# Summing 27 conditioning chunks on VectorE inside the 512-token feed-forwards of a two-block transformer kernel

## What is computed

```python
mod_x = (jax.nn.silu(c) @ w_ada[l] + b_ada[l]).reshape(bn, 1, N_MOD, d)
mod_c = (jax.nn.silu(c_ctx) @ w_ada[l] + b_ada[l]).reshape(1, 1, N_MOD, d)
h_x = _half_ffn(h_x, norm_g[l, 0], mod_x[:, :, 0], mod_x[:, :, 1], mod_x[:, :, 2], ffn1_up[l], ffn1_down[l])
...
h_x = h_x + mod_x[:, :, 5] * (jnp.concatenate([o_a, o_b, o_c], axis=-1) @ w_out[l])
h_x = _half_ffn(h_x, norm_g[l, 2], mod_x[:, :, 6], mod_x[:, :, 7], mod_x[:, :, 8], ffn2_up[l], ffn2_down[l])
```

## Time and profile before

| | us |
|---|---|
| median of 3 runs | 2213.01 |
| profiled execution | 2216.32 |
| its span, first to last instruction | 2215.0 |
| TensorE matmuls busy | 2140.7 |
| VectorE busy | 1074.3 |
| ScalarE busy | 770.6 |
| mean granted TensorE clock (1.0 is 2.4 GHz) | 0.978 |

### The profile page before, as it was taken

The page is one execution under the profiler, slowest core; times in us unless marked ns, Lnnn a source line. Parts: engine busy times, 40 slices in busy tenths (PEclk is TensorE's granted clock), DMA queues, the critical chain, the costliest instruction groups (busy, mean ns, idle before and its releaser), DMA issues. The chain is left out here.

```text
span 2215.0 us, 41069 instructions
## 1 busy us (share of the span) xinstructions
PE 2140.7 (97%) x17886; PEld 1844.7 (83%) x17886; DVE 1074.3 (49%) x1570; ACT 770.6 (35%) x1094; POOL 60.3 (3%) x59
## 2 busy tenths in 40 slices
PE   7998899999999999989999999999999999899998
PEld 7887699998888888867788888888888888779998
DVE  5654765565333335676453333354333335755555
ACT  5331444453222223236332222233222223355433
POOL 0000030000000000220000000000000000200000
PEclk9998899999999999999999999999999999999999
DMA  7516644543323224337422232232232225254543
GB/s 283 198 63 236 240 175 164 195 173 115 147 90 116 95 78 127 91 117 285 172 99 94 84 114 95 79 140 78 89 109 95 83 97 153 96 193 168 174 174 111
DMA packets 56627, 303.57 MB, mean 137 GB/s; under 512 B 13728, under 2 KB 17184, under 8 KB 27552
## 3 DMA queue, kind: packets, MB, share of 16 engines
q1 hardware_dynamic: 56480, 301.40, 38.8%
HBM read 300.33 MB, written 1.05 MB: 136 GB/s over the span
## 5 line engine op out<-in xcount | busy, mean ns | idle before, releaser
L459 PE MATMUL ps<-a_hi,w_hi 128*128 128x512 f32 (+1 forms) x1992 | 683.5, 343 | 1.7 <-DVE w_lo L446 1.5
L460 PE MATMUL ps<-a_lo,w_hi 128*128 128x512 f32 (+1 forms) x1992 | 678.0, 340 | 0.0
L461 PE MATMUL ps<-a_hi,w_lo 128*128 128x512 f32 (+1 forms) x1992 | 677.8, 340 | 0.0
L446 DVE TENSOR_TENSOR w_lo<-raw,w_hi 128x2048 fp32r<-128x2048 f32 (+2 forms) x230 | 470.1, 2047 | 207.7 <-ACT w_hi L440 207.4
L440 ACT ACTIVATE w_hi<-raw 128x2048 fp32r<-128x2048 f32 (+2 forms) x229 | 391.2, 1715 | 234.2 <-PE ps L461 174.3
L459 PEld LDWEIGHTS ps<-a_hi,w_hi 128*128 128x128 f32 x1992 | 377.8, 190 | 47.9 <-issue 3.6
L461 PEld LDWEIGHTS ps<-a_hi,w_lo 128*128 128x128 f32 x1992 | 378.0, 190 | 42.2
L460 PEld LDWEIGHTS ps<-a_lo,w_hi 128*128 128x128 f32 x1992 | 378.0, 190 | 41.8
L459 PE MATMUL ps<-ff_hi,w_hi 128*128 128x512 f32 (+1 forms) x880 | 306.5, 348 | 3.6 <-DVE w_lo L446 3.2
L460 PE MATMUL ps<-ff_lo,w_hi 128*128 128x512 f32 (+1 forms) x880 | 304.9, 347 | 0.0
L461 PE MATMUL ps<-ff_hi,w_lo 128*128 128x512 f32 (+1 forms) x880 | 304.9, 346 | 0.0
(11 more groups left out here) (356 smaller groups left out, 1829.4 us busy)
## 6 DMA issues: line engine op xcount, KB each, us to landing
raw<-in_w_gu SPq DMA_DIRECT2D x110, 1024.0 KB, 4.8
raw<-in_w_ada SPq DMA_DIRECT2D x72, 1024.0 KB, 5.2
raw<-in_w_dn SPq DMA_DIRECT2D x80, 704.0 KB, 4.0
raw<-in_w_in SPq DMA_DIRECT2D x26, 1024.0 KB, 4.9
raw<-in_w_out SPq DMA_DIRECT2D x12, 1024.0 KB, 5.4
direct<-in_w_cmp SPq DMA_DIRECT2D x4, 1024.0 KB, 6.9
h<-in_x SPq DMA_DIRECT2D x2, 1024.0 KB, 7.1
nb<-in_rpb SPq DMA_DIRECT2D x32, 64.0 KB, 7.4
```

Of the source, the lines that this page charges most:

```text
L446: nc.vector.tensor_tensor(w_lo[slot][:, cols], raw[b][:, cols], w_hi[slot][:, cols].bitcast(F32), ALU.subtract).then_inc(lo_ready if done ...
L459: nc.tensor.matmul(banks[m], w1, a1, start=start and k == 0, stop=False)
L460: nc.tensor.matmul(banks[m], w1, a2, start=False, stop=False)
L461: last = nc.tensor.matmul(banks[m], w2, a1, start=False, stop=stop and k == pr.kt - 1)
```

## The change

The attentions hold fewer conditioning chunks: 10 in place of 24 in attention 0, and 2 in place of 10 in attention 1; the one in the norm before the second layer's projection goes. Three feed-forwards of 512 tokens (the first and the last of layer 0 and the first of layer 1) hold nine each, beside every second gu chunk: 4 in the first half, 5 in the second. The four that the first feed-forward held beside its chunks 3 to 6 are now four of these nine. That makes 27 chunks, and they are no longer multiplied by TensorE from `raw`. For each of the two inputs VectorE adds up over the eight row blocks: block times its column of `silu_c` (one number for each partition), plus the sum so far. The sum of input 0 goes to a tile of its own, `ada_sum`, and that of input 1 over the chunk's first row block. Then TensorE adds over the partitions: two rounds of four matmuls with a constant matrix `pick` that is one in the column of the input and zero elsewhere. The fold of a chunk stands ahead of the product of the next gu chunk; its drain follows it on VectorE. The slot in `raw` is free after the fold.

```diff
-INNER = {"w_out": (1, 8), "w_out_0": (2, 24), "w_out_1": (2, 10), "w_gu": (2, 1), "w_gu1_0": (2, 1), "w_in_0": (2, 1),
-         "w_gu2_0": (2, 1), "w_gu1_1": (2, 1), "w_in_1": (2, 1)}
+INNER = {"w_out": (1, 8), "w_out_0": (2, 10), "w_out_1": (2, 2), "w_gu": (2, 1), "w_gu1_0": (2, 1), "w_in_0": (2, 1),
+         "w_gu2_0": (2, 1), "w_gu1_1": (2, 1)}
+STREAM = {0: (0, 2, 4, 6), 1: (0, 2, 4, 6, 8)}
...
-            add_gu(f"w_gu1_{l}", T2, half, range(4) if l == 0 and half == 0 else ())
+            add_gu(f"w_gu1_{l}", T2, half, STREAM[half])
...
-            add_gu(f"w_gu2_{l}", t, half)
+            add_gu(f"w_gu2_{l}", t, half, STREAM[half] if t == T2 else ())
...
+    def fold_ada(pe, a, b):
+
+        pe.wait_ge(ada_summed, KT * 2 * (streamed.index(a) + 1))
+        for w in range(2):
+            for g in range(4):
+                c = slice(32 * g, 32 * (g + 1))
+                at = raw[ada_slot[a]][:, 0:2 * P] if w else ada_sum[:]
+                last = nc.tensor.matmul(b[c].rearrange("p (m f) -> p m f", m=2), pick[:, w, :],
+                                        at.rearrange("p (m f) -> p m f", m=2)[:, :, c], start=w == 0, stop=w == 1,
+                                        tile_position=(0, 32 * g))
+        last.then_inc(ada_mult, 1)
+
+    def sum_ada(dve, pr, k):
+
+        a = pr.ada(k)
+        turn, slot = pr.loaded(k, 0, 1)
+        n = KT * 2 * streamed.index(a)
+        dve.wait_ge(landed[slot], 16 * (turn + 1))
+        wait(dve, ada_mult, a)
+        for j in range(KT):
+            x = raw[slot][:, j * 2 * P:(j + 1) * 2 * P]
+            for w, to in enumerate((ada_sum[:], raw[slot][:, 0:2 * P])):
+                c = silu_c[:, j, w:w + 1]
+                if j:
+                    dve.wait_ge(ada_summed, n - 1)
+                    last = nc.vector.scalar_tensor_tensor(to, x, c, to, ALU.mult, ALU.add)
+                else:
+                    wait(dve, ada_summed, n)
+                    last = nc.vector.tensor_scalar(to, x, c, None, ALU.mult)
+                last.then_inc(ada_summed, 1)
+                n += 1
...
-            if first + k in pr.ada_at:
-                pe.wait_ge(ada_drained, pr.ada(first + k))
-                multiply_ada(pe, pr.loaded(first + k, 0, 1), ps[6][:, 0:64])
+            if first + k - 1 in pr.ada_at:
+                a = pr.ada(first + k - 1)
+                pe.wait_ge(ada_drained, a)
+                fold_ada(pe, a, ps[6][:, 0:64])
...
-            if head + k in pr.ada_at and evac_ada is not None:
-                evac_ada(pr.ada(head + k))
             if k or pr.name not in ("w_out_0", "w_out_1"):
                 split(c + 1, pr.loaded(head + k + 1, r), (slot + 1) % RING, pr.size)
+            if evac_ada is not None and pr.ada_at:
+                evac_ada(pr, k)
...
+        def stream(pr, k):
+            if k in pr.ada_at:
+                sum_ada(dve, pr, k)
+            if k - 1 in pr.ada_at:
+                stream_drain(dve, pr.ada(k - 1))
```

More of the change, by code:

```diff
@@ L405, in program @@
     ada_drained = sem("ada_drained")
+    ada_summed = sem("ada_summed")
     ada_turned = sem("ada_turned")
@@ L410, in program @@
     products = plan()
+    streamed = [pr.ada(k) for pr in products for k in pr.ada_at]
+    ada_slot = {pr.ada(k): pr.loaded(k, 0, 1)[1] for pr in products for k in pr.ada_at}
     gu_before = {}
@@ L664, in staged @@
         c = pr.end - 1
-        if pr.n - 1 in pr.ada_at and evac_ada is not None:
-            evac_ada(pr.ada(pr.n - 1))
+        if evac_ada is not None and pr.ada_at:
+            evac_ada(pr, pr.n - 1)
         if pr.ahead is not None:
@@ L818, in dve_product @@
             dve.wait_ge(sq_cleared, norm_serial(pr.squares) + 1)
+        def stream(pr, k):
[3 more added lines that the diff above has]
+                stream_drain(dve, pr.ada(k - 1))
         if pr.name == "w_out":
             dve.wait_ge(lo_ready, pr.base + 1)
-        staged(dve, pr, split, evac, chained[pr.base], lambda a: stream_drain(dve, a))
+        staged(dve, pr, split, evac, chained[pr.base], stream)
     squared = {pr.squares: pr for pr in products if pr.squares is not None}
@@ L1078, in program @@
           [temp("xf2", [P, 8, 32], at_rs), temp("xf3", [P, 8, 32], at_sq)]]
+    ada_sum = place("ada_sum", [P, S], F32, cursor[0])
     hc = place("hc", [P, 4, 2 * NCMP], F32)
@@ L1081, in program @@
     vct = place("vct", [P, 2, HD], F32)
+    pick = place("pick", [P, 2, 32], F32)
     at_rope = cursor[0]
@@ L2510, in _ @@
         nc.vector.memset(silu_c[:], 0.0).then_inc(silu_c_cleared, 1)
+        step(nc.vector.memset(pick[:], 0.0))
+        for w in range(2):
+            last = nc.vector.memset(pick[:, w, w:w + 1], 1.0)
+        step(last)
         dve.wait_ge(consts_loaded, 32)
```

## The result

| | time, median | span of the profiled execution |
|---|---|---|
| before | 2214.5 us (2210.8 to 2218.2, 6 runs) | 2215.0 us |
| after | 2264.5 us (2259.7 to 2270.4, 6 runs) | 2265.5 us |

What follows compares the result with a forecast made beforehand. TensorE was taken to bound the kernel: -28.8 us of multiplies removed, +10.8 folds, +24.5 late sums, +18.9 late loads make +25.4, so 2238.4 us against the median of 2213.0; range 2207 to 2266 us, forecast's chance 0.50.

Steps and rivals of the forecast that it cites:

- the clock: Rival: at the new feed-forward waits the granted clock falls, 1.7 us each; 2259 us at half the fold places; chance 0.12.
- no overlap: Rival: VectorE's sum instructions don't overlap, so 16 take 7.4 us and waits grow 1.2 us in 24 places; 2267 us; chance 0.05.
- What bounds the kernel: Whole kernel: TensorE, busy 97% of the span; work taken off pays where it runs without a gap.
- Multiplies removed in the feed-forward: First feed-forward of layer 0: four ada multiplies of 1.26 us each go, -5.0 us.
- Attention 0: Last fourteen steps of attention 0 lose their ada multiplies; 2.25 us a step, saving 16.5 us (bounds 8 and 20).
- Attention 1: Steps 5 to 12 of attention 1 lose eight ada multiplies, 0.9 us each: -7.2 us (5 to 8).
- The half-attention rival: Rival: attention gives half of its 23.7 us, because the chain there, not TensorE, sets the step; 2250 us; chance 0.13.
- The fold: Feed-forwards: 8 added matmuls for each of 27 ada chunks, 0.4 us each (0.3 to 0.5): +10.8 us.
- VectorE's sums late: Before folds: sums of 6.2 us end late; TensorE waits 1.5 us in 3 places, 0.95 in 21: +24.5 us.
- VectorE keeps up: Rival: VectorE starts an instruction each 0.27 us and keeps up, but the load doesn't; 2214 us, no change; chance 0.08.
- The load late: Weight chunks queued behind the ada load awaiting its slot: TensorE waits 0.9 us in 21 places, +18.9 us (14 to 28).
- Unrolled loops at nothing: Feed-forward products: unrolling their loops costs nothing, since unrolled and looped ones run at the same 10.88 us a chunk.

Runs made afterwards that it cites:

- both mends: Fold in the middle of the next gu chunk and ada load behind its weight chunk: on the changed kernel 2214.1 us, on it with its last part undone 2211.4 us.
- Both: The changed kernel with the fold in the middle of the next gu chunk and each ada chunk loaded behind its weight chunk: 2214.1 us, ratio 1.0003.
- the four other kernels with its code: The changed kernel with half of the sum, with the load behind, with the fold in the middle, and with both: 2243.1, 2253.4, 2419.8 and 2214.1 us.
- half of the sum: The changed kernel with VectorE summing only four of eight row blocks, so the conditioning vectors are incomplete: 2243.1 us, ratio 1.0129.
- the last part undone: The changed kernel with ten ada chunks in attention 1 and one in the norm again, none in the third feed-forward, which is looped again: 2242.0 us, ratio 1.0126.
- more on ScalarE and VectorE: Two kernels: the changed kernel with one more ScalarE instruction in each attention step, 2274.2 us, or one more VectorE instruction, 2270.2 us.
- the kernel with the load behind: The changed kernel with each streamed ada chunk loaded behind the weight chunk of its number instead of ahead of it: 2253.4 us, ratio 1.0187.
- the kernel with the fold in the middle: The changed kernel with the fold in the middle of the next gu chunk, after 8 of its 16 tiles, load order unchanged: 2419.8 us, ratio 1.0924.

## Why the forecast had the sign and half of the size

The measured 2264.5 us lie just inside the range of 2207 to 2266, but the change is twice the forecast one. The 25 us that it missed are, in the trace of after: 7.5 less gained in the attentions, 6.2 for the folds, 5.7 for restarts behind the load waits, 1.7 of the clock, 1.0 of load waits, less 2.5 for the sums. The rest, 5 to 6 us, stays open. One sign that the prediction gave for itself being wrong came: the clock fell inside a feed-forward, once. The range was wide at its upper end for the sake of rivals (the clock, no overlap) that did not come true; that it held is luck.

- **What bounds the kernel; that a wait of TensorE costs its length: right.** The two kernels with both mends stand 1 us above and 5 below before, those with waits 25 to 207 us above.
- **Multiplies removed in the feed-forward, -5.0: right.** In "Both" the half with four folds more and four multiplies less shrank by 2.3 us, one with four folds more grew by 2.5: the multiplies were 4.8.
- **Attention 0, -16.5: -13.2.** I took 2.25 us a step, from 1.9 us of ScalarE's and of VectorE's busy time and a little for the chain. The steps take 2.48, since ScalarE's row of work and the wait behind it don't overlap. Nine steps make 2.1 of the 3.3 us.
- **Attention 1, -7.2: -3.0, and only -1.0 to -1.3 in the four other kernels with its code.** This is the step that failed worst. I took 3.1 us a step for TensorE without the multiply and "the chain takes a little"; in after two steps take 7.19 and 7.57 us, with TensorE idle for up to 1.24 us for a copy of ScalarE (line 1978). In the four others a fall of the clock behind these waits takes 1.6 us more; I had the clock as a rival for the feed-forwards only. Two steps of after, columns as above:

```profile
2004.30:2011.50 7.20, 5.34 (x49) 3.08 (x48) 4.97 (x12) 5.37 (x13) 0.00 (x0) 1.00 0.00 0
```

```profile
2007.63 0.63 PE L1917 MATMUL ps<-consts_sb,ee 128*128 128x128 f32 x4 [1.24 <-ACT pt L1978]
```

  No engine is busy for more than 5.37 of 7.20 us. What TensorE waits for is ScalarE's copy, and what ScalarE waits for is VectorE's maximum (2.32 us above), which needs TensorE's scores: a chain over three engines, where my estimate was one engine's work. The half-attention rival (2250 us) named this mechanism, for both attentions; it came true in attention 1 only.
- **The fold, 27 x 0.4 = 10.8: 27 x 0.63 = 17.0.** Of the 0.23 us missing, 0.11 are the start of the large matmuls behind it: the first takes 0.34 us to the next, not 0.23. The rest was sized too low.
- **VectorE's sums late, +24.5: +22.0,** each by its own step. The rival "VectorE keeps up" is out. So is "no overlap", although its 2267 us lie nearest to the result: by the rule in the Trainium skill, VectorE: DVE Perf Modes, section The DRAIN you can't avoid, the sum would take 7.4 us and these waits 2.1; the trace has 6.28 and 0.9. The prediction read this section too narrowly: it also says that an operation which is not held starts earlier, and these instructions did. A total that fits is no evidence for a mechanism.
- **The load late, +18.9: 19.9 in idle rows, and 25.5 in time.** A wait costs more than its row shows: the idle time is counted from the end of the matmul before, which lies 0.16 us behind the start of the next one in a full stream, and the first matmul after it takes 0.11 more. 21 x 0.27 = 5.7. (For the folds both are in the 0.63.) The 0.9 was right as a mean only: in 13 of 21 places the second transfer landed 6.8 to 7.1 us after its issue and the wait is 0.4 to 0.7; in two it landed after 7.3 and 7.4 (0.9 and 1.1 us), in six after 8.0 to 8.4 (1.6 to 2.0 us).
- **The clock, given 0.12.** In after it fell in the feed-forwards once for 44 waits, behind one of 1.81 us, and cost 1.7 us (1343.0 to 1346.4 below, columns as above). This is less than its price: with the 1.7 us VectorE caught up, and the next fold had no wait of 0.87 us. In all five kernels with load waits of this length, 17 of these waits lasted 1.8 us or more, and the clock fell behind eight of them (once in after, twice with half of the sum, never with the last part undone, twice and three times with more on ScalarE and VectorE), and behind none of the others, nor behind the 24 folds that waited 1.6 us in the kernel with the load behind. In the kernel with the fold in the middle it fell at each wait. So the rival's mechanism exists; at the waits of this change it took little. The Trainium skill, TensorE: Matmul & The Clock Gate, section What's actually happening, has idleness bring the half clock; the runs agree for the long waits and for few of the short.

```profile
1343.00:1346.40 3.40, 3.40 (x10) 2.57 (x10) 1.60 (x3) 2.43 (x2) 0.00 (x0) 0.53 0.00 0
```

- **The sum of the halves:** -5.0 + 17.0 + 22.0 + 19.9 + 5.7 + 1.7 = 61.3 against 62.8 measured. With attention's 7.5 us less gain, the 62.8 hold 21 of the 25 us missed; the rest, 2.6 before the first feed-forward and 1.7 at the last norm, isn't explained by the change. At the last norm and the projection behind it the granted clock fell three times in after and once in before; the kernel with the last part undone has the code of before there, three falls, and 3.5 us more than before.
- **Unrolled loops at nothing: right** by themselves. But see the next section.

**The slow landings.** Two bursts in after, their stretches of the DMA queues (kind: packets, MB, share) and TensorE's wait behind each:

```profile
q1 hardware_dynamic: 374, 2.81, 87.9%
q8 instruction: 1, 0.02, 0.7%
```

```profile
1732.79 0.50 PE L463 MATMUL ps<-a_hi,w_hi 128*128 128x512 f32 x1 [2.00 <-DVE w_lo L450]
```

The other, 25.6 us later:

```profile
q1 hardware_dynamic: 375, 2.81, 88.8%
```

```profile
1756.98 0.50 PE L463 MATMUL ps<-a_hi,w_hi 128*128 128x512 f32 x1 [0.59 <-DVE w_lo L450]
```

In after, 8 of the 21 bursts have a packet of the instruction queue among those of the weights; they are the eight that landed after 7.3 us or later. The 13 others have none, or (one) a packet in their last 0.2 us. The kernel with half of the sum has nine such bursts of 21, at 7.3 to 8.4 us. TensorE waits for the second load of each such burst, so the packet goes with 0.4 to 1.5 us of its time. This is a coincidence of rows; no kernel here took the packets away.

## What to carry to other kernels

Before work is moved into a stage, look there for the order of each queue and for who releases each buffer: here the work itself cost TensorE 17 us and its two waits 48, and two edits of order took the waits away. Cost a spared instruction by the chain that remains without it, engine by engine in order of time, not by the busiest engine's sum, and read the granted clock in that stretch too: one more fall in attention 1 was worth as much as half of what the change gained there. And give each new wait the restart behind it besides the idle time that its row will show.

## What was new of the hardware

- A 1 MB transfer, second in its burst, landed 6.8 to 7.1 us after its issue in 13 of 21 bursts, and 7.3 to 8.4 us in the eight where one 16 KB packet of instructions fell among it.
- The first large matmul after a wait or after a few small ones takes 0.34 us to the next in place of 0.227, at a granted clock of 1.00.
- In waits of TensorE of 5.8 to 7.4 us the granted clock was at half before the wait ended, and 2.9 to 6.2 us of the work behind it ran at half. Behind waits of 1.8 to 2.0 us it fell in eight of 17 places.
- In attention 1, with waits of 1.23 and 0.62 us in one step, the clock fell in the four kernels from "Half of the sum" to "Both" and not in after; it cost 1.6 us.
